# Mixing the two maps of a difference-attention head on GpSimd, and both maxima in one instruction

## The reference

```python
def diff_attend(q, k, v, lam):
    s = jnp.einsum('bqhmd,bkhmd->bhmqk', q * (DIFF_HD ** -0.5), k)
    p = jax.nn.softmax(s.astype(jnp.float32), axis=-1)
    a = (p[:, :, 0] - lam * p[:, :, 1]).astype(v.dtype)
    return jnp.einsum('bhqk,bkhd->bqhd', a, v)
```

## Time and profile before

| | |
|---|---|
| Three runs, median (lowest to highest) | 2495.7 us (2493.99 to 2499.58) |
| Profiled execution, span of its instructions | 2494.9 us |
| PE busy | 2422.2 us, 97% |
| DVE busy | 1438.8 us, 58% |
| ACT busy | 1197.7 us, 48% |
| GpSimd busy | 29.0 us, 1% |
| Mean granted TensorE clock | 0.997 |
| DVE maxima, L2114 | 240 instructions, 139.1 us |
| DVE mixing, L2145 | 48 instructions, 483 to 753 ns |

### The profile page before, as it was taken

The page is one execution under the profiler, slowest core; times in us unless marked ns, Lnnn a source line. Parts: engine busy times, 40 slices in busy tenths (PEclk is TensorE's granted clock), DMA queues, the critical chain, the costliest instruction groups (busy, mean ns, idle before and its releaser), DMA issues.

```text
span 2494.9 us, 33717 instructions
## 1 busy us (share of the span) xinstructions
PE 2422.2 (97%) x12949; PEld 2007.3 (80%) x12949; DVE 1438.8 (58%) x2461; ACT 1197.7 (48%) x2288; POOL 29.0 (1%) x54
## 2 busy tenths in 40 slices
PE   6999999899999999899999999999999998999999
PEld 4877788677788878788887888878888887888887
DVE  3453244674348644565547677665679846555565
ACT  4552223653137432475336555464466555544643
POOL 2000000000000000000000000000000000000000
PEclk9999999999999999999999999999999999999999
DMA  7312342114331132142521531655555661655554
GB/s 237 102 43 80 123 161 92 51 53 159 114 106 44 43 129 90 51 140 83 179 77 43 177 119 53 187 193 174 180 169 176 195 186 42 202 178 173 186 169 135
DMA packets 164768, 317.89 MB, mean 127 GB/s; under 512 B 10455, under 2 KB 22609, under 8 KB 164097
## 3 DMA queue, kind: packets, MB, share of 16 engines
q1 hardware_dynamic: 161552, 303.67, 38.7%
q0 software_dynamic: 3056, 12.06, 1.7%
HBM read 312.55 MB, written 3.15 MB: 127 GB/s over the span
## 4 chain that ended last, share of the span: by engine, by line
PE 88%; DVE 6%; ACT 3%; issue 2%; DMA 1%; SPq 0%; DVEq 0%; ACTq 0%
PE bank L843 24%; PE bank L845 23%; PE bank L844 23%; PE bank L888 6%; PE bank L1014 5%; DVE neg_max L2114 2%; PE bank L976 1%; PE bank L873 1%; DVE w_low_part L1702 1%; PE bank L987 1%; PE bank L1075 1%; ACT w_high_part L1217 1%; PE bank L914 1%; DMA x<-in_x_dram 0%; PE bank L993 0%
## 5 line engine op out<-in xcount | busy, mean ns | idle before, releaser
L1702 DVE TENSOR_TENSOR w_low_part<-w_raw,w_high_part 128x1024 fp32r<-128x1024 f32 (+3 forms) x544 | 636.9, 1186 | 601.7 <-ACT w_high_part L1217 599.1
L1217 ACT ACTIVATE w_high_part<-w_raw 128x1024 fp32r<-128x1024 f32 (+3 forms) x544 | 551.9, 1031 | 692.1 <-PE bank L845 561.4
L843 PE MATMUL bank<-w_high_part,h_high 128*128 128x512 f32 (+3 forms) x2128 | 819.7, 385 | 9.5 <-DVE h_low L2003 3.1
L845 PE MATMUL bank<-w_high_part,h_low 128*128 128x512 f32 (+3 forms) x2128 | 807.6, 380 | 0.0
L844 PE MATMUL bank<-w_low_part,h_high 128*128 128x512 f32 (+3 forms) x2128 | 807.0, 379 | 0.0
L843 PEld LDWEIGHTS bank<-w_high_part,h_high 128*128 128x128 f32 x2128 | 401.2, 189 | 92.5 <-issue 12.2
L845 PEld LDWEIGHTS bank<-w_high_part,h_low 128*128 128x128 f32 x2128 | 400.8, 188 | 74.9
L844 PEld LDWEIGHTS bank<-w_low_part,h_high 128*128 128x128 f32 x2128 | 401.5, 189 | 70.5 <-issue 0.2
L1525 ACT ACTIVATE stage<-bank,neg_max 128x512 f32<-128x512 f32 (+1 forms) x240 | 147.3, 616 | 128.6 <-DVE neg_max L2114 70.7
L888 PE MATMUL bank<-ident,stage 128*128 128x128 f32 (+1 forms) x1112 | 166.8, 277 | 8.7 <-ACT probs_turned L1645 2.4
L888 PEld LDWEIGHTS bank<-ident,stage 128*128 128x128 f32 (+1 forms) x1112 | 126.6, 139 | 59.5 <-issue 42.9
(11 more groups left out here) (296 smaller groups left out, 2412.2 us busy)
## 6 DMA issues: line engine op xcount, KB each, us to landing
w_raw<-in_w_in_dram SPq DMA_DIRECT2D x160, 512.0 KB, 3.8
w_raw<-in_a_w_in_dram SPq DMA_DIRECT2D x96, 512.0 KB, 4.0
w_raw<-in_b_w_in_dram SPq DMA_DIRECT2D x80, 512.0 KB, 4.6
w_raw<-in_w_branch_dram SPq DMA_DIRECT2D x48, 512.0 KB, 4.3
w_raw<-in_w_mod_dram SPq DMA_DIRECT2D x40, 512.0 KB, 5.0
w_raw<-in_a_w_out_dram SPq DMA_DIRECT2D x32, 512.0 KB, 4.5
w_raw<-in_c_w_in_dram SPq DMA_DIRECT2D x32, 512.0 KB, 3.9
w_raw<-in_w_out_dram SPq DMA_DIRECT2D x16, 512.0 KB, 3.7
```

Of the source, the lines that this page charges most:

```text
L843: pe.matmul(o, high, wh, start=(k == 0), stop=False)
L845: mm = pe.matmul(o, low, wh, start=False, stop=(k == u.kt - 1))
L1217: nc.scalar.activation(WH[:, n % PART_SLOTS, 0:kt, 0:width], raw[:, 0:kt, 0:width], ACT.Copy).then_inc(*S.up("w_high", c))
L1702: v.tensor_tensor(WL[:, s, 0:kt, 0:width], raw[:, 0:kt, 0:width], WH[:, s, 0:kt, 0:width].bitcast(F32), ALU.subtract).then_inc(*S.up("w_lo ...
```

## The change

- The mixing leaves DVE. `combine` ends with the ratio, and a new function `mix_maps` on GpSimd multiplies the second map by it and, after a wait for that instruction, adds the product to the first. The signal "maps_mixed" takes the place of "spare_read" for PE's transposes and for ACT's second exponential two items later.
- DVE waits for the scores of both maps and takes both maxima in one instruction over two neighbouring banks. For that the eight banks become one tensor, and PE's turn is moved on by one where the first bank of a pair would have an odd number.
- GpSimd's other loads keep their order; the mixing of each layer stands ahead of the loads that followed. ACT's head norm gets a wait for the last mixed item.

```diff
--- before.py
+++ after.py
@@ -501,7 +501,8 @@
         TRIL = SMASK[:, 0, :]
         assert top[0] <= nc.sbuf_usable_end, (top[0], nc.sbuf_usable_end)
 
-        banks = [ctx.enter_context(nc.psum_tensor(f"bank{b}", [P, 512], F32)) for b in range(8)]
+        all_banks = ctx.enter_context(nc.psum_tensor("bank", [P, 8, 512], F32))
+        banks = [all_banks[:, b, :] for b in range(8)]
         POOL = {"wide": (0, 1, 2, 3), "turn": (4, 5), "out": (6, 7), "turn4": (4, 5, 6, 7)}
 
         def stage(n):
@@ -516,6 +517,12 @@
 
         def ps(key):
             return banks[S.bank(key)[0]]
+
+        def ps_two(first, second):
+
+            a, b = (S.bank(first)[0], S.bank(second)[0]) if S.known else (0, 1)
+            assert b == a + 1, (first, a, b)
+            return all_banks[:, a:a + 2, :]
 
         def q_low(l, r, h, n, t):
 
@@ -697,6 +704,18 @@
             def rows(name, src, at, count, which):
                 load(ROWS[at:at + count, which, :], src, "rows_landed")
 
+            def mix_maps(l, qt):
+
+                for n, (t, h) in enumerate(items(l, 1, qt)):
+                    nk = P * len(key_tiles(t))
+                    p0, p1 = stage(n)[:, 0:nk], spare(n)[:, 0:nk]
+                    pool.wait_ge(*S.at("map_ratio", (l, t, h)))
+                    nc.gpsimd.tensor_scalar(p1, p1, CC[:, n % 4, 1:2], None,
+                                            ALU.mult).then_inc(*S.up("map_scaled", (l, t, h)))
+                    pool.wait_ge(*S.at("map_scaled", (l, t, h)))
+                    nc.gpsimd.tensor_tensor(p0, p0, p1, ALU.add).then_inc(*S.up("maps_mixed", (l, t, h)))
+                    S.same("probs", (l, 1, t, h), "maps_mixed")
+
             rows("b_mod", dram["b_mod"].rearrange("l (k p) -> (l k) p", p=P), VEC["b_mod"], 48, 0)
             rows("norm_g", dram["norm_g"].rearrange("l (k p) -> (l k) p", p=P), VEC["norm_g"], 16, 0)
             rows("q_norm", dram["mla_q_norm"].rearrange("l (k p) -> (l k) p", p=P), VEC["q_norm"], 6, 0)
@@ -724,6 +743,7 @@
                 for j in range(2):
                     pool.wait_ge(*S.emptied((("t", 0, 0, j), t)))
             load(acc_spill, ACC[:, :, :].rearrange("p t d -> p (t d)"), "acc_saved")
+            mix_maps(0, ALL_TILES)
             for m in range(2):
                 pool.wait_ge(*S.filled(("s", 0, 1, ALL_TILES[-1], DH - 1, m)))
             pool.wait_ge(S.sem("acc_saved"), 16)
@@ -734,6 +754,7 @@
                 x = dram["ctx"] if t in CTX_TILES else dram["x"]
                 load(X[:, t, :], x[0, P * (t % 2):P * (t % 2) + P, :], f"x{t}_back")
 
+            mix_maps(1, LAT_TILES)
             for h in (SH - 2, SH - 1):
                 pool.wait_ge(*S.filled(("s", 1, 2, LAT_TILES[-1], h, 0)))
             load(BMASK[:, :, :], dram["k_b_mask"].rearrange("g p f -> p g f"), "b_mask_landed")
@@ -977,7 +998,10 @@
                                       start=True, stop=True).then_inc(*fills(b))
                         elif r == 1 or h % 2 == 0:
                             halves = [(h, 0), (h, 1)] if r == 1 else [(h, 0), (h + 1, 0)]
-                            two = [take("turn4" if i < FIRST else "wide", ("s", l, r, t, hh, m)) for hh, m in halves]
+                            pool = "turn4" if i < FIRST else "wide"
+                            if r == 1:
+                                turns[pool] += turns[pool] % 2
+                            two = [take(pool, ("s", l, r, t, hh, m)) for hh, m in halves]
                             hq, hk = (h, h) if r == 1 else (h // 2, h // 4)
                             q_high, k_high = QH[:, hq, P * t:P * t + P], KH[:, hk, 0:nk]
                             ql = q_low(l, r, hq, 1, t).rearrange("p a c -> p (a c)")
@@ -1520,7 +1544,11 @@
                             act.wait_ge(*S.filled(("pt", l, r, *todo[i - ring])))
                         for m in range(MAPS[r]):
                             key = ("s", l, r, t, h, m)
-                            dst = probs_at(r, i) if m == 0 else take_spare()
+                            dst = probs_at(r, i) if m == 0 else spare(i)
+                            if m and i < 2:
+                                act.wait_ge(*S.nth("spare_read", spares[0]))
+                            elif m:
+                                act.wait_ge(*S.at("maps_mixed", (l, *todo[i - 2])))
                             act.wait_ge(*S.at("neg_max", key))
                             nc.scalar.activation(dst[:, 0:nk], ps(key)[:, 0:nk], ACT.Exp, bias=NM[:, i % 8, m:m + 1],
                                                  accum_out=LS[:, t % 2, m, h:h + 1]).then_inc(*S.empties(key))
@@ -1551,6 +1579,7 @@
 
             def head_norm(l, qt):
                 load_table(ACT.Sqrt)
+                act.wait_ge(*S.at("maps_mixed", (l, qt[-1], DH - 1)))
                 act.wait_ge(*S.at("head_variance", l))
                 nc.scalar.activation(STAT[:, 1, 8 * qt[0]:32], STAT[:, 1, 8 * qt[0]:32],
                                      ACT.Sqrt).then_inc(*S.up("head_deviation", l))
@@ -2103,7 +2132,14 @@
                     if i < len(todo):
                         t, h = todo[i]
                         nk = P * len(key_tiles(t))
-                        for m in range(MAPS[r]):
+                        if r == 1:
+                            maps = [("s", l, 1, t, h, m) for m in range(2)]
+                            for key in maps:
+                                dve.wait_ge(*S.filled(key))
+                            v.tensor_reduce(NM[:, i % 8, 0:2], ps_two(*maps)[:, :, 0:nk], AX_X, ALU.max,
+                                            negate=True).then_inc(*S.up("neg_max", maps[0]))
+                            S.same("neg_max", maps[1], "neg_max")
+                        for m in range(MAPS[r]) if r != 1 else ():
                             key = ("s", l, r, t, h, m)
                             dve.wait_ge(*S.filled(key))
                             s = ps(key)
@@ -2139,13 +2175,8 @@
                 dve.wait_ge(*S.emptied(("s", l, 1, t, h, 1)))
                 dve.wait_ge(*S.emptied(("s", l, 1, t, h, 0)))
                 link(v.reciprocal(c[:, 0:1], LS[:, t % 2, 1, h:h + 1]))
-                link(v.scalar_tensor_tensor(out=c[:, 1:2], in0=LS[:, t % 2, 0, h:h + 1],
-                                            scalar=NLAM[:, l:l + 1], in1=c[:, 0:1], op0=ALU.mult, op1=ALU.mult))
-                p0 = stage(n)[:, 0:nk]
-                v.scalar_tensor_tensor(out=p0, in0=spare(spares[0])[:, 0:nk], scalar=c[:, 1:2], in1=p0,
-                                       op0=ALU.mult, op1=ALU.add).then_inc(*S.up("spare_read", ("p1", l, t, h)))
-                S.same("probs", (l, 1, t, h), "spare_read")
-                spares[0] += 1
+                v.scalar_tensor_tensor(out=c[:, 1:2], in0=LS[:, t % 2, 0, h:h + 1], scalar=NLAM[:, l:l + 1],
+                                       in1=c[:, 0:1], op0=ALU.mult, op1=ALU.mult).then_inc(*S.up("map_ratio", (l, t, h)))
 
             def outputs(l, r, t, g):
                 n = GROUP[r]
```

## The result

The changed kernel took 2508.97 us (median of 4 runs, 2507.18 to 2511.09) against 2494.84 for the kernel before, run beside it. The ratio is 1.0053, 95% interval 1.0041 to 1.0066. The forecast was 2490.0 and a range of 2487.5 to 2501. The time came out beyond the range, on the other side of no change. The profiled execution took 2507.18 us and spans 2505.4, against 2494.9 before.

What follows compares the result with a forecast made beforehand. DVE was taken to bound the 256-key steps, DVE and PE to be level with 512 keys. Gains of 1.7, 1.45, 1.4 and 1.15 made 5.7 us off 2494.9; with 0.8 for the median, 2490.0, range 2487.5 to 2501.

Steps and rivals of the forecast that it cites:

- the term for GpSimd's scaling: GpSimd's multiplication of the second map by the ratio: 0.60 us with 512 keys, since one read and one write can overlap.
- The addition: GpSimd's adding of the scaled second map to the first: 1.15 us with 512 keys, as it must read two operands.
- The pair: GpSimd's scaling and addition for one item: 1.75 us with 512 keys, 0.95 with 256; bounds 1.05 to 2.32.
- DVE's relief: Mixing leaves DVE in 48 difference-attention items: 27.8 us of DVE removed, only part of it on the path.
- The one maximum: Both maps' maxima in one DVE instruction: 1.13 us instead of 1.20 with 512 keys, 0.60 instead of 0.66 with 256.
- The later start: First exponentials wait for both maxima: each chain starts 0.25 to 0.55 us later, not covered at a stretch's start.
- The handovers: Two handovers for GpSimd's instructions add 0.1 us each, making its step 1.95 with 512 keys and 1.15 with 256.
- The sum over the stretches: Layer 0's three stretches gain 1.7, 1.45 and 1.4 us, layer 1's gains 1.15; together 5.7.
- The latency: An item's way from scores to mixed map takes some 6.1 us, due after some 7: under 1 us to spare.
- GpSimd becomes the bound: Rival: GpSimd's two instructions, with DVE's ratio joining the loop, take 2.78 us per 512-key item; 2503 us, chance 0.20.
- Its turning point: The rival decides from about 2.1 us for GpSimd's two instructions under the exclusion, or 2.5 without.
- The exclusion: DVE instructions with two SBUF inputs and GpSimd ones reading SBUF block each other; alone it would cost under 1 us.

## Why the prediction was wrong

**The step that failed is the term for GpSimd's scaling.** It was put at 0.60 us for 512 keys, between 0.52 and 0.95, and measured 1.56 where undisturbed (504 to 512 us; mean 1.59). Even the upper bound was too low. It counted passes at a memset's rate (204 ns for 128 elements), and the argument that one read and one write overlap had no row behind it. The same product takes 1.04 in another form, so an instruction's form has a price that no count of passes gives. The addition was put at 1.15, between 0.52 and 1.37, and takes 1.28: near, and inside. The pair takes 2.84, above the upper bound of 2.32 for both; with 256 keys 0.92+0.73 = 1.65 against 0.95. With the scaling at 1.56 the prediction's own step would have been 1.56+1.15+0.2 = 2.91, over PE's 2.37. That is the distance measured, but that it fits to the hundredth is luck: the addition took 0.13 more and the handovers some 0.1 less.

The prediction leant here on the Trainium skill as a support beside its own sum: page "GPSIMD Engine Reference", section "Performance versus the Vector engine". Its two-input figure, scaled to 1.15 to 1.2 as an estimate, is near the measured 1.28. The near-line-rate for one input, from which it had 0.5, stands in the same page's section "Engine selection" and was not borne out for this form: 1.56, and 1.04 for the same product with two inputs.

**DVE's relief** was right in the main: 26.2 us off its busy time. That DVE was 9.53 of 15 us busy in 500 to 515 (forecast: some 10) is no proof, since the items came at 2.91; at 2.37, with the scaling taken out, it was 10.65.

**The one maximum** was right. With 512 keys DVE goes on 1.14 us after its start:

```profile
484.00 1.23 DVE L2139 TENSOR_REDUCE neg_max<-bank 128x2 f32<-128x1024 f32 x1 [0.23 <-PE bank L1017]
485.14 0.15 DVE L2177 RECIPROCAL map_ratio<-row_sums 128x1 f32<-128x1 f32 x1
```

The forecast was 1.13. With 256 keys it is 0.61 (470.37 to 470.98), forecast 0.60. The later start cost 0.57 in layer 1 (forecast 0.5); in layer 0, where the sum had nothing for it, items 2 to 6 took 5.59 instead of 5.36 with only the one maximum.

**The handovers**, 0.1 each, were right or high: scaling to addition 0.09 (506.01+1.56 to 507.66), addition to the next scaling none. The pair's distance was to be 1.95 and is 2.91.

**The sum over the stretches** was right for a quick GpSimd: without the scaling all four stretches come within 0.6 us of the forecast, and the kernel gains 8.7 us by its ratio, 7.6 by the spans of the profiles, where 5.7 were forecast.

**The latency** of 6.1 us had under 1 us to spare, and the pair costs 1.1 more than was put. Where GpSimd has every second item only, the weight loads of PE's transposes still waited for it 12 times, 8.0 us in all, in 455 to 535 us: the single item comes late.

**The rival** "GpSimd becomes the bound", at 0.20, is what came. That GpSimd sets the pace, the places (transposes and second exponentials) and the sign were right; the size was short. It had 57.3 us for items 6 to 31 and 34.7 for layer 1, where 59.8 and 37.0 were measured. That its 2.78 an item is near the 2.91 is in part luck: the pair costs 2.84 and not 2.32, but the ratio did not join the loop, where the rival had 0.26 for it, and one of the two handovers was none. Its turning point held: with the product as a `tensor_tensor` the pair is 1.04+1.28 = 2.32, between the 2.1 and 2.5 given, and the kernel is level with the one before.

**The exclusion** between DVE and GpSimd was rightly named, and small in the changed kernel, mostly because of when the ratio comes. The ratio's instruction has two SBUF inputs, and in 35 of the 48 items it starts well inside GpSimd's scaling, with 0.06 us and more of that still to run. In all 35 it takes its 0.22 us:

```profile
503.10 1.57 POOL L713 TENSOR_SCALAR stage<-stage,map_ratio 128x512 f32<-128x512 f32 x1
504.22 0.22 DVE L2178 SCALAR_TENSOR_TENSOR map_ratio<-row_sums,neg_lam,map_ratio 128x1 f32<-128x1 f32 x1
```

Seven times the ratio is stretched, to between 0.33 and 1.28 us. In five of the seven it begins inside an addition and ends with it; in the other two (476.02 and 483.01) the two begin at nearly the same time. A weight split of DVE that begins inside a scaling (1349.76) takes its 1.22 us too; the addition behind it (1350.19) is then held up, 1.91 us instead of 1.28. Two more holds, the first by a weight split:

```profile
487.39 1.21 DVE L1731 TENSOR_TENSOR w_low_part<-w_raw,w_high_part 128x1024 fp32r<-128x1024 f32 x1
487.57 2.47 POOL L713 TENSOR_SCALAR stage<-stage,map_ratio 128x512 f32<-128x512 f32 x1
...
495.91 1.27 POOL L716 TENSOR_TENSOR stage<-stage 128x512 f32<-128x512 f32 x1
...
495.93 1.28 DVE L2178 SCALAR_TENSOR_TENSOR map_ratio<-row_sums,neg_lam,map_ratio 128x1 f32<-128x1 f32 x1
```

The weight split pushes a scaling from 1.56 to 2.47 (0.9 us on GpSimd, which is the bound). The ratio's stretch at 495.93 costs only about 0.1: GpSimd's next scaling starts at 497.30, and its addition ends at 497.18. The rule of the Trainium skill, page "SBUF — State Buffer", section "Who interferes with whom", has a DVE instruction with two SBUF inputs contend with any GpSimd one that reads SBUF. The traces agree for GpSimd's additions, in both directions: whichever engine came second was held up, and the form with one input was not. For GpSimd's scaling they agree in one direction only: behind DVE's weight split it was held up, but it never held up the ratio. There the measurement decides, and no run here says why.

**What stays open.** Why the `tensor_scalar` form costs more on GpSimd than the same product with two inputs was not found. That the clock's falls in the changed kernel cost little of their own, since GpSimd was busy meanwhile, is argued from its windows only (1.92 of 2 us busy in 492 to 494); no run took them out there. In the first fall GpSimd was not full (1.58 of 2 us in 468 to 470): its scalings begin at 465.84, 467.69 and 469.75, where they can follow each other in 1.71, so some 0.5 us there may be the clock's. In the kernels that share the items, the exclusion, the clock and the longer way were not separated. The 8.7 us without scaling are 1.7 more than its two stages gained (7.0), which is within that ratio's interval.

## What to carry to other kernels

A sum that moves work to an engine whose arithmetic no row shows is only as good as its bounds, and a bound made of passes isn't an upper bound: ask at what price the engine becomes the pacemaker, here about 2.4 us an item, and measure one instruction of each form first. Before an operation goes to GpSimd, try its other forms: `tensor_tensor` with a repeated column did in 1.04 us what `tensor_scalar` did in 1.56. Split between engines (the cheap half on DVE, 0.49, the addition on GpSimd, 1.28) the same idea won 0.3%. In a pipeline that is only just ahead of its due times, a longer way through a slow engine can cost even when only every second item takes it: the transposes waited for it 12 times.

## What the runs showed of the hardware

- GpSimd, fp32, 128 partitions, from SBUF to SBUF, for 512 and 256 elements: `tensor_scalar` with a factor for each partition 1.56 and 0.92 us, with a constant 1.49 and 0.85; `tensor_tensor` addition 1.28 and 0.73; `tensor_tensor` product with one operand repeated 1.04 and 0.61 (all undisturbed). DVE's `tensor_scalar` of 512 takes 0.49.
- An instruction of one element in each partition on DVE waited out a GpSimd addition (0.22 us became 0.86 and 1.28), because it has two SBUF inputs; written with one tensor input and two pointer scalars it took 0.27 to 0.28 each time.
- The same DVE instruction in its two-input form was not held up by GpSimd's `tensor_scalar`: 35 times it began inside one and took 0.22 us, and 32 and 27 times more in the kernels with the mixing alone and with the constant. The other way round, a GpSimd `tensor_scalar` behind a DVE subtraction of 128x1024 with two SBUF inputs took 2.47 us instead of 1.56.
- After waits of 1.57 and 1.29 us, with 1 us of work between them, TensorE's granted clock fell to 0.50 in 1328 to 1335 us, which made one item 2 us longer. With eight needless transposes in the first wait (0.68 and 1.30 us), or with waits of 1.57 and 0.68 us, it stayed at 1.00.
